# One chunk later: moving the weight rounding of ScalarE and VectorE behind the attention and scan steps of a mixer

## The reference, cut to what matters

```python
qa, ka, va, zb, xbc, dtb, qc, kc, vc, gpre = jnp.split(h @ w_in, SPLIT_POINTS, axis=-1)
o_a = _diff_attention(qa, ka, va, diff_lambda, diff_subln_g, layer)   # 8 heads of two maps
o_b = _mamba2(zb, xbc, dtb, ...)                                      # convolution, scan, 16 heads
o_c = _stick_breaking(qc, kc, vc)                                     # 16 heads
branches = jnp.stack([o_a, o_b.astype(h.dtype), o_c], axis=2)
proj = jnp.einsum('bsrc,rcd->bsrd', branches, w_branch)
gates = jax.nn.sigmoid(gpre.reshape(b, s, N_BRANCH, D_MODEL) + gate_bias)
return jnp.einsum('bsrd,bsrd->bsd', gates, proj) @ w_out
```

```python
log_stay = jnp.where(strict, jax.nn.log_sigmoid(-z), 0.0)
after = lax.cumsum(log_stay, axis=3, reverse=True) - log_stay
a = jnp.where(strict, jnp.exp(jax.nn.log_sigmoid(z) + after), 0.0)
out = jnp.einsum('bhqk,bkhd->bqhd', a, v)
```

## Time and profile before

| | |
|---|---|
| three runs | 2498.25, 2500.4, 2504.82 us (median 2500.4) |
| profiled execution | 2500.21 us, its span 2498.1 us |
| mean granted TensorE clock | 0.941 of full speed |
| TensorE busy | 2279.3 us, 91% of the span |
| VectorE busy | 1660.5 us, 66% |
| ScalarE busy | 1152.8 us, 46% |
| GpSimd busy | 356.2 us, 14% |
| mixer of layer 1, third and fourth stretch | about 380 to 650 us |
| mixer of layer 2, the same | about 908 us later |

### The profile page before, as it was taken

One profiled execution on the slowest core, in us unless ns is written; L12 is line 12 of the kernel. 1 busy time (PEld: TensorE's weight loads), 2 busy tenths in 40 slices (PEclk: granted clock), 3 DMA queues, 4 the chain that ended last, 5 costly groups with the idle time before them and its releaser, 6 DMA issues.

```text
span 2498.1 us, 33499 instructions
## 1 busy us (share of the span) xinstructions
PE 2279.3 (91%) x12480; PEld 1925.2 (77%) x12480; DVE 1660.5 (66%) x2142; ACT 1152.8 (46%) x1658; POOL 356.2 (14%) x143
## 2 busy tenths in 40 slices
PE   7998998889989989989988899899978947999999
PEld 6886888768868878878877678688777836887887
DVE  6765665478767756766664578667666554667997
ACT  4443454364444434434553554444444123546785
POOL 3431000000015413411000000054201010000000
PEclk9998998889989989999998999999989857999999
DMA  8765543234657747756442345577632000658996
GB/s 298 240 211 148 169 134 108 88 121 132 192 173 238 223 140 246 234 161 181 143 137 76 93 140 164 168 220 234 204 103 71 3 1 6 231 188 262 361 360 231
DMA packets 320169, 426.86 MB, mean 171 GB/s; under 512 B 28192, under 2 KB 220080, under 8 KB 320032
## 3 DMA queue, kind: packets, MB, share of 16 engines
q1 hardware_dynamic: 315904, 412.45, 51.8%
q0 software_dynamic: 4016, 12.56, 1.8%
q10 hardware_dynamic: 112, 0.04, 0.0%
HBM read 423.90 MB, written 1.05 MB: 170 GB/s over the span
## 4 chain that ended last, share of the span: by engine, by line
PE 77%; DVE 7%; ACT 6%; issue 5%; DVEq 2%; DMA 1%; PEld 1%; POOL 1%; POOLq 0%; ACTq 0%; PEldq 0%; SPq 0%
PE ps L267 18%; PE ps L269 18%; PE ps L268 18%; PE ps L514 10%; PE ps L3171 4%; ACT hi L250 3%; DVE lo L254 2%; PE ps L300 2%; PE ps L1056 1%; ACT room L932 1%; DVE room L1141 1%; PE ps L505 1%; DMA raw<-in_w_up 1%; DVEq L1098 1%; DVEq L733 1%
## 5 line engine op out<-in xcount | busy, mean ns | idle before, releaser
L254 DVE TENSOR_TENSOR lo<-raw,hi 128x1024 fp32r<-128x1024 f32 x737 | 1020.8, 1401 | 605.7 <-ACT hi L250 599.5
L250 ACT CAST hi<-raw 128x1024 fp32r<-128x1024 f32 x737 | 768.2, 1047 | 864.1 <-PE ps L269 690.9
L267 PE MATMUL ps<-hi,xT_hi 128*128 128x512 f32 (+2 forms) x1440 | 574.7, 399 | 5.6 <-issue 4.9
L269 PE MATMUL ps<-hi,xT_lo 128*128 128x512 f32 (+2 forms) x1440 | 563.1, 391 | 0.0
L268 PE MATMUL ps<-lo,xT_hi 128*128 128x512 f32 (+2 forms) x1440 | 562.1, 390 | 0.0
L267 PEld LDWEIGHTS ps<-hi,xT_hi 128*128 128x128 f32 x1440 | 279.4, 194 | 58.7 <-issue 6.5
L269 PEld LDWEIGHTS ps<-hi,xT_lo 128*128 128x128 f32 x1440 | 278.2, 193 | 56.8
L268 PEld LDWEIGHTS ps<-lo,xT_hi 128*128 128x128 f32 x1440 | 279.3, 194 | 51.4
L684 POOL TENSOR_SCALAR room<-room,vecs 128x1536 f32<-128x1536 f32 x28 | 131.4, 4692 | 232.6 <-DMA room<-in_w_ada 232.6
L267 PE MATMUL ps<-xT_hi,hi 128*128 128x256 f32 x544 | 160.5, 295 | 0.0
L268 PE MATMUL ps<-xT_lo,hi 128*128 128x256 f32 x544 | 155.0, 285 | 0.0
(11 more groups left out here) (531 smaller groups left out, 3214.4 us busy)
## 6 DMA issues: line engine op xcount, KB each, us to landing
raw<-in_w_mix_in SPq DMA_DIRECT2D x368, 256.0 KB, 2.9
raw<-in_ffn_w_in SPq DMA_DIRECT2D x352, 256.0 KB, 3.4
raw<-in_ffn_w_out SPq DMA_DIRECT2D x176, 256.0 KB, 2.9
raw<-in_w_gate SPq DMA_DIRECT2D x128, 256.0 KB, 4.5
raw<-in_w_up SPq DMA_DIRECT2D x128, 256.0 KB, 6.2
raw<-in_w_down SPq DMA_DIRECT2D x128, 256.0 KB, 5.1
room<-in_w_ada SPq DMA_DIRECT2D x32, 768.0 KB, 6.1
raw<-in_w_branch SPq DMA_DIRECT2D x96, 256.0 KB, 3.0
```

The source lines that it names most:

```text
L250: nc.scalar.copy(hi[c.hi_slot][:, 0:c.cols], raw[c.slot][:, 0:c.cols]).then_inc(rounded, 1)
L254: nc.vector.tensor_tensor(lo[c.slot][:, 0:c.cols], raw[c.slot][:, 0:c.cols], hi[c.hi_slot][:, 0:c.cols], ALU.subtract).then_inc(split, 1)
L267: pe.matmul(out, a[0], b[0], start=start, stop=False)
L269: return pe.matmul(out, a[1], b[0], start=False, stop=stop)
```

## The change

In the third and the fourth stretch, ScalarE and VectorE handle at odd h the chunk before the current one. The end of a block (evacuation, bias, branch product, sigmoid of the gates) comes first at the half, one chunk later than before; then the steps of attention and scan as they stood; and the tick last, for the chunk before. At h = 1 of the third stretch there is none. The last tick of the third stretch is done at half 1 of the fourth, that of the fourth ahead of the fifth. A's second branch product moves between the two loops on VectorE, B's second bias behind the loop. TensorE's, GpSimd's and SyncE's queues are unchanged. The diff, with both engines' loops:

```diff
--- before.py
+++ after.py
@@ -1607,9 +1607,8 @@
 
             third = self.grid(self.third)
             for h in range(2 * len(third)):
-                b, c = third[h // 2]
-                if h % 2:
-                    tick_act(act, b.chunks[c])
+                b, c = third[h // 2 - 1]
+                if h % 2 and h > 1:
                     gates_of_last(b, c)
                     if c + 1 == len(b.chunks) and b not in self.A.gate + self.A.branch:
                         if b is self.xbc[0]:
@@ -1657,12 +1656,14 @@
                     scan.act_exp(act, 0)
                 elif h == 73:
                     scan.act_exp(act, 1)
+                if h % 2 and h > 1:
+                    tick_act(act, b.chunks[c])
 
             fourth = self.grid(self.fourth)
+            before = third[-1:] + fourth
             for h in range(2 * len(fourth)):
-                b, c = fourth[h // 2]
+                b, c = before[h // 2]
                 if h % 2:
-                    tick_act(act, b.chunks[c])
                     gates_of_last(b, c)
                 if h == 2:
                     self.turns_c[0].act(act)
@@ -1676,7 +1677,11 @@
                     self.turns_b[0].act(act)
                 elif h == 38:
                     self.turns_b[1].act(act)
-
+                if h % 2:
+                    tick_act(act, b.chunks[c])
+
+            b, c = fourth[-1]
+            tick_act(act, b.chunks[c])
             for n, (b, c) in enumerate(self.grid(self.fifth)):
                 tick_act(act, b.chunks[c])
                 gates_of_last(b, c)
@@ -1717,9 +1722,8 @@
 
             third = self.grid(self.third)
             for h in range(2 * len(third)):
-                b, c = third[h // 2]
-                if h % 2:
-                    tick_dve(dve, b.chunks[c])
+                b, c = third[h // 2 - 1]
+                if h % 2 and h > 1:
                     if c + 1 == len(b.chunks):
                         if b in self.A.branch:
                             self.A.dve(dve, self.A.branch.index(b))
@@ -1771,12 +1775,15 @@
                     scan.dve_exponents(dve, 1)
                 elif h == 73:
                     scan.dve_weights(dve, 0)
-
+                if h % 2 and h > 1:
+                    tick_dve(dve, b.chunks[c])
+
+            self.A.dve(dve, 1)
             fourth = self.grid(self.fourth)
+            before = third[-1:] + fourth
             for h in range(2 * len(fourth)):
-                b, c = fourth[h // 2]
+                b, c = before[h // 2]
                 if h % 2:
-                    tick_dve(dve, b.chunks[c])
                     if c == 3 and b in self.C.branch:
                         self.C.dve(dve, self.C.branch.index(b))
                     for m in (self.C, self.B):
@@ -1813,7 +1820,12 @@
                     self.turns_b[0].dve(dve)
                 elif h == 38:
                     self.turns_b[1].dve(dve)
-
+                if h % 2:
+                    tick_dve(dve, b.chunks[c])
+
+            self.B.dve_bias(dve, 1)
+            b, c = fourth[-1]
+            tick_dve(dve, b.chunks[c])
             for n, (b, c) in enumerate(self.grid(self.fifth)):
                 tick_dve(dve, b.chunks[c])
                 if c == 3:
```

## The result

The changed kernel takes 2458.93 us (median of four runs, 2456.77 to 2459.70) against 2499.32 us (four runs, 2497.17 to 2504.82): 0.983 of the time before, interval 0.9813 to 0.9846. The forecast was 2473.7, in a range from 2460 to 2488.

The account below looks back on a forecast made before the run. TensorE's work plus its idle time was taken to set the end. Terms 11.1 + 1.0 + 4.4 - 4.4 + 1.2 + 0 = 13.3 us a mixer, 26.6 for two, took 2500.4 to 2473.7, range 2460 to 2488.

Parts of the forecast that it names:

- What bounds the kernel: Whole kernel: TensorE, busy 91% of the span, sets the end by its work plus idle time; both mixers alike.
- the ring: Weight chunks, one shallower: five chunks (14 us) stand ahead of TensorE, longest hold some 7 us; cost put at nothing.
- Attention, pairs 1 to 6: Third stretch, stick-breaking attention: nine TensorE waits vanish, with the display time behind them; gain 11.1 us a mixer.
- First sums: Attention's first sum products: power and splits end 1.6 us earlier, an evacuation of 0.6 comes ahead; gain 1.0 of 4.3.
- Pair 7 and the convolution: End of third stretch: sums wait about 4 us, decays' wait falls from 3.4 to about 2.4; block 4.4 us shorter.
- Turn: Into the fourth stretch: C's transposes wait 5.3 us instead of 0.97 for A's last branch product; loss 4.4 a mixer.
- Rest of the fourth stretch: Scan quads 2 and 3: VectorE's chain of about 16 us fits TensorE's 18, L1261's wait goes; gain 1.2 a mixer.
- Clock: TensorE's half-clock stretches around waits: unknown, bounded between -2.5 and +2.6 us a mixer, taken as 0.
- Rival 1: The clock follows the waits: each mixer +2.6, pair 7 keeps full clock (1.5); 8 us more, 2465; chance 0.12.
- Rival 2: Even pairs keep half their waits: cast behind a step waiting for VectorE, split behind that cast; 2486; chance 0.18.
- Rival 3: The turn costs nothing new: the wait at 575.86 stays about 1 us; 2465; chance 0.06.
- Rival 4: Slower: cast behind exponential behind exponents at three more places, quads and pair 7; +7.4 a mixer, 2515; chance 0.05.

Follow-up runs that it names:

- third stretch alone: The changed kernel with the fourth stretch as before the change, the owed round and split done between the two: 2461.72 us, 0.9835 of the kernel before.
- ScalarE alone: The kernel before, with the tick moved to the tail of the odd half on ScalarE only, VectorE as before: 2538.97 us, 1.016.
- the turn repaired: The changed kernel with A's last branch product on VectorE moved ahead of quad 0's weights and the last tick: 2444.37 us, 0.977 of the kernel before.
- pair 7's stay step first: The kernel of VectorE alone, with pair 7's stay step on VectorE ahead of the split of half 43: 2445.5 us, 0.9775.
- VectorE alone: The kernel before, with the tick moved to the tail of the odd half on VectorE only, ScalarE as before: 2445.3 us, 0.9772.
- the last version: VectorE alone, plus ScalarE's weights of the odd pairs ahead of the cast and pair 7's stay step ahead of the split: 2444.19 us, 0.9771.

## Why the prediction was wrong, and where it was right

*What bounds the kernel.* Right: what moved the time was TensorE's waits in the mixers with the clock, and both mixers did the same. No wait for L254 appeared in them, so the ring was deep enough one chunk shallower.

*Attention, pairs 1 to 6.* Right in the waits. Forecast 11.1; idle time gone 9.7 and 1.5 of display. All nine waits went, those of L1070 and of the transposes of A among them. That the lag was not needed for it, nor the order if there was the lag, I had not seen.

*First sums.* Right: 4.3 to 3.3.

*Pair 7 and the convolution.* Forecast 4.4, measured 4.0. The sums' wait is 4.0 as forecast. The wait for the decays is 1.2 and not 2.4, without effect on the sum: VectorE sets the end of the block, and it came 20.7 us after the split of pair 7 (494.4 to 515.07) where I had 20.5. The 2.4 does not follow from my own terms: before, TensorE needed 22.0 us from the sums of pair 7 to the transposes of x, 3.4 of them wait, so 18.6 of its own; added to 512.1 that is 530.7, 1.1 us ahead of the 531.8 that I gave VectorE. I had TensorE arrive too early.

*Turn.* Right: 5.0 against 5.3, loss 4.0 against 4.4, by the chain that the prediction names.

*Rest of the fourth stretch.* Right: 1.1 against 1.2.

*Clock.* This is the step that failed, and only in size: the sum has a 0 for the clock, between -2.5 and +2.6 a mixer. Measured: +4.5 in the pairs, +2.6 behind the transposes of x, +1.7 in the last interval, -2.7 behind the new wait, in all +6.1, or 12.2 us for two mixers of the 15 that the forecast was short. As a check, the granted clock over the whole stretch, before and after:

```profile
387.40:641.90 254.50, 230.76 (x1239) 194.28 (x1239) 169.21 (x258) 115.64 (x137) 7.65 (x7) 0.91 0.38 117
```

```profile
387.00:622.00 235.00, 221.50 (x1238) 189.28 (x1238) 168.76 (x258) 115.34 (x138) 7.52 (x7) 0.93 0.41 129
```

(the first is of the kernel before). At 1.2 GHz ran 0.09 x 254.5 x 2 = 46 us and now 0.07 x 235 x 2 = 33: 13 fewer, at most 6.5 us. The other 2.6 us of the 15 are the 1.7 from outside the mixers and a kernel before whose median, with a fourth run, is 1.1 us lower than the 2500.4 I started from.

Four things were wrong in the working. First, only the stretch from 400 to 500 was credited. There the clock gave 4.5, inside the 5.1 that I allowed, and the turn took 2.7 where I had 2.5; by these two alone the clock's sum, +1.8, would have stayed inside my bounds. What broke them is the 2.6 behind the transposes of x and the 1.7 of the last interval, for which the working has no term. The row at 536.20 in the earlier trace rows, eight small transposes in 1.97 us, against eight in 1.06 at 575.86, shows the clock near half behind the 3.4 us wait, and I shortened that wait without asking what the clock behind it would do. Second, the new 5.3 us wait was charged its 2.5 (it is 2.7), while the waits that went were not credited by the same measure. Third, I chose the middle of the two bounds, with the argument that the narrow products stay; they stay, and 10.3 us of half clock with them, but the granted clock of the pairs rose from 0.87 to 0.90 nevertheless. Fourth, the 5.1 was no upper bound. A clock of 0.85 over 45 us means 13.5 us at 1.2 GHz, which cost 6.7 if TensorE works all the while, and 0.88 over 55 us costs 6.6; I halved the first once more and the second twice. That the 4.5 fell inside it is luck, the more so as it can be out by 2 us (third stretch alone).

Of the clock's terms, the 2.6 behind the transposes of x and the -2.7 behind the turn are shown by experiment to follow TensorE's wait there. For the 4.5 in the pairs only the rows speak, and why the last interval gained 1.7 is open.

*The rule of the Trainium skill* ("TensorE: Matmul & The Clock Gate", section "A second HAM failure mode: psum-queue depth-cycling"), that brief idles between groups of matmuls make the clock swing and cost throughput: the runs agree at the transposes of x (clock 0.72 behind 3.4 us) and at the turn (0.56 behind 5.0 us), and it was the better guide. I gave it the upper end, 2.6 a mixer; the clock gave 6.1. It does not cover the 10.3 us of half clock that no wait precedes.

*The rivals.* Rival 1 (the clock follows the waits, 2465, chance 0.12) names what happened, and it too was priced too low. Rival 2 (waits move): no even pair kept a wait. Rival 3: the turn cost what it was said to. Rival 4: not in this change, but real at one quad in the kernel with ScalarE alone, where rival 2's chain is real too.

## What to carry to other kernels

When two engines in a row supply a third, put the supplier's part first at each step and the consumer's last: here that alone gave 0.977, the reverse 1.016, and both moved together (0.980), lagged (0.980) or both at once (0.983) less, though the last, with the turn repaired, is at 0.977 too. A wait of the matmul engine can have two prices, its length and a half-clock stretch behind it; read the second from the same instructions at full clock elsewhere in the trace (1.06 against 1.97 us for eight transposes), and credit a wait that goes as you charge one that comes. Two edits that cure the same wait should be tried one by one: here either alone was 7 us better than both, with intervals of the ratio that just overlap.

## What was not expected of the hardware

Needless work made the kernel faster: 14 products nobody reads, in a wait of 3.4 us of both mixers, gave 0.9962 (0.9949 to 0.9974). The interval behind the transposes of x shows the same thing in every kernel: 7.3 to 7.5 us where the wait ahead of it was 0.3 to 1.5, 8.95 where it was 2.0, 9.9 to 10.2 where it was 2.9 to 5.4. Two kernels had 8.1 and 8.4, and that is not clock. The transposes wait there a second time, for ScalarE's part of the convolution, and this second wait lies inside the interval. The kernel with pair 7's stay step first:

```profile
515.34 0.66 PE L1224 MATMUL ps<-consts,room 128*128 128x128 f32 x4 [0.61 <-DVE small L1309]
...
516.52 0.66 PE L1224 MATMUL ps<-consts,room 128*128 128x128 f32 x4 [0.53 <-ACT room L1151]
```

And two microseconds of a mixer are hard to see in the time. Between VectorE alone and the last version the profiled executions differ by 6.9 us (spans 2443.8 and 2436.9): 1.4 and 3.4 in the mixers, 2.0 outside. Yet the medians differ by 1.1 us, since the executions of either kernel lie 6 to 10 us apart, and the last version's profiled one is its fastest. The stretches outside the mixers, where no version changes anything, add up to between 1984.7 and 1990.4 us in the thirteen profiles. What moves them is open.
